# One of four sample tiles gets its first expert products from gathered rows and VectorE dots

## The chip, the cores and the metric

The kernel runs on one core of a Trainium2 chip. The metric is the device time of one launch in microseconds. Times are the median of several executions; the profile is one further execution. The engines are TensorE (PE; its weight loads are PEld), VectorE (DVE), ScalarE (ACT), GpSimd (POOL) and SyncE (SP), which issues most transfers.

## The reference

One layer runs for a prompt of 128 tokens and a sample of 512 tokens: adaLN modulation, a long-convolution half and a gated-linear-attention half, an output projection, then the PEER expert mixer. The change is in the mixer:

```python
def peer_ffn(h, wq, sub_keys, u_tab, v_tab):          # h2 of 128 + 512 tokens, D = 1024
    q = (x @ wq).reshape(T, 8, 2, 128)
    s = einsum('thpd,hpkd->thpk', q, sub_keys)         # 128 sub-keys per half
    s_top, i_top = top_k(s, 16)
    cand_s = s_top[:, :, 0, :, None] + s_top[:, :, 1, None, :]
    best, pos = top_k(cand_s.reshape(T, 8, -1), 16)    # 16 experts of 16384 for each of 8 heads
    gate = softmax(best)
    ...
    a = gelu(einsum('td,tkd->tk', xt, u_tab[it]))      # 128 experts per token
    return einsum('tk,tkd->td', gt * a, v_tab[it])
```

All data is float32. Each token uses 8 x 16 = 128 of the 16384 experts; a row of `u_tab` or `v_tab` is 1024 numbers.

## The kernel before

There are five tiles of 128 tokens: tile 0 is the prompt, tiles 1 to 4 the sample. After the mixing half come, in order:

- **The query product** (L878, L879): the moving operand is 320 tokens wide, in a three-part split of each float32 (high by high, high by low, low by high). While it runs, DVE takes the top keys.
- **Stage A**, `BLK_A` = 40 blocks. A block is 128 experts. All 16384 experts, 128 blocks, are multiplied with the 512 sample tokens: `first_products` (L898 and on) makes 24 matmuls 128x512 a block (L906), after ACT has rounded the expert rows to `uhi` (L1672) and POOL has made the rest `ulo` (L1815). ACT takes the gelu of the block (L1682) to `aout`, which SP stores to `gelu_scratch` and then loads the rows of four blocks on. Meanwhile DVE finishes the top-k (`best_keys`, `best_experts`), first of the prompt, whose expert numbers `idx0` POOL waits for ahead of its ninth split; it issues four row gathers there.
- **Stage B**, 4 x 16 blocks. Besides the same products, PE makes one 128x128 product per sample token (L946) that scatters the token's 128 gates over its 16384 experts. DVE builds one operand `eA` of these (L1442, 8 a block) and ACT the other, `eB` (L1708, L1710); ACT copies the result to `gst`, which SP stores to `gate_scratch`. DVE now makes `ulo` too (L1417). For the prompt nothing is dense: POOL gathers the rows `u[idx]` of the 128 prompt tokens, one expert a token at a time (L1827, 128x1024), and DVE takes the dot with `h2row` (L1427), `DOTS_B` = 2 a block, 128 in all.
- **Stage C**, the remaining 24 blocks: only the first products.
- **Stage 2**, 128 blocks, 24 matmuls 128x512 a block (L965): gelu value times gate for 512 tokens (DVE L1459), its high and low parts, the high and low parts of the `v` rows, and the product. For the prompt POOL gathers a row of `v_tab` a token and DVE adds it (L1475), one a block.

Each engine works through its list in the order written; semaphores join them. Buffers that matter here: `ugat` and `vgat` have `GSLOT` = 4 slots (the gather of dot g+4 is issued once dot g is done), `uraw`, `vraw` and `ain` have four, `gin` holds four blocks' gates and there are two of it, `uhi` and `ulo` have two.

## Time and profile before

| | us |
|---|---|
| median of 3 executions | 2248.36 (2241.95 to 2249.47) |
| profiled execution, its own time | 2244.61 |
| its span | 2242.8 |
| mean granted clock of TensorE, share of full | 0.979 |

| engine | busy us | share of the span |
|---|---|---|
| PE | 2154.6 | 96% |
| DVE | 1388.6 | 62% |
| ACT | 834.1 | 37% |
| POOL | 508.7 | 23% |

The 16 transfer engines moved 475.50 MB. In the chain that ended last PE has 90% of the span: L965 (stage 2) 30%, L906 (first products) 29%, L946 (gate scatter) 5%. A share over the whole span says little here, because the stages have different limits; the rows below take one stage at a time. Times in them count from the start of the span.

### The profile page before, as it was taken

The numbers are of one execution on the slowest core, as the hardware profiler recorded it, in microseconds if no ns is written. First come the engines' busy times: TensorE is split into PE (matmuls) and PEld (weight loads), VectorE is DVE, ScalarE is ACT, GpSimd is POOL, SyncE is SP. The second block draws the span as 40 slices with busy tenths as digits, with TensorE's granted clock in tenths as the row PEclk, the third lists the DMA queues.
The fourth block names the chain that finished last, engine by engine and source line by source line (L and its number), as shares of the span: only waits on it lengthen the run. The fifth ranks groups of instructions, "written<-read, shape, count | busy, mean of one in ns | idle before, by whom it ended". The sixth has DMA issues, their size and how long they took to land.

```text
span 2242.8 us, 28983 instructions
## 1 busy us (share of the span) xinstructions
PE 2154.6 (96%) x9868; PEld 1664.0 (74%) x9868; DVE 1388.6 (62%) x2919; ACT 834.1 (37%) x1506; POOL 508.7 (23%) x329
## 2 busy tenths in 40 slices
PE   6999999698998999999999999999999999999998
PEld 2554455445997787788888888887888888888886
DVE  4221425423889999677777777226666666666665
ACT  2111003323212222677877877223222223223222
POOL 0000001002324555333333332003222222222120
PEclk8999999798999999999999999999999999999999
DMA  9121114305102444488888887747888888888883
GB/s 338 53 75 45 73 43 178 150 1 197 56 21 85 169 136 142 160 307 317 322 319 315 317 319 293 285 139 281 315 298 284 290 293 285 293 283 296 279 298 132
DMA packets 179297, 475.50 MB, mean 212 GB/s; under 512 B 16263, under 2 KB 50215, under 8 KB 176648
## 3 DMA queue, kind: packets, MB, share of 16 engines
q1 hardware_dynamic: 142344, 340.20, 42.7%
q0 software_dynamic: 36864, 134.23, 17.9%
q8 instruction: 42, 0.69, 0.1%
q14 instruction: 47, 0.39, 0.1%
HBM read 401.76 MB, written 72.61 MB: 212 GB/s over the span
## 4 chain that ended last, share of the span: by engine, by line
PE 90%; DVE 4%; DMA 2%; ACT 1%; issue 1%; POOL 1%; SPq 0%; POOLq 0%; DVEq 0%; ACTq 0%
PE ps L965 30%; PE ps L906 29%; PE ps L624 5%; PE ps L946 5%; PE ps L717 3%; PE ps L843 3%; PE ps L878 3%; PE ps L879 3%; PE ps L683 2%; DMA wring<-in_w_ada 1%; PE ps L623 1%; PE ps L636 1%; DMA ain<-gelu_scratch 1%; PE ps L742 1%; PE ps L743 1%
## 5 line engine op out<-in xcount | busy, mean ns | idle before, releaser
L906 PE MATMUL ps<-h2hi,uhi 128*128 128x512 f32 x1024 | 446.3, 436 | 18.5 <-DVE scores L1375 7.7
L965 PE MATMUL ps<-vhi,whi 128*128 128x512 f32 x1024 | 400.8, 391 | 8.1 <-DVE wlo L1465 8.1
L906 PE MATMUL ps<-h2hi,ulo 128*128 128x512 f32 x1024 | 402.8, 393 | 0.0
L906 PE MATMUL ps<-h2lo,uhi 128*128 128x512 f32 x1024 | 401.1, 392 | 0.0
L965 PE MATMUL ps<-vlo,whi 128*128 128x512 f32 x1024 | 400.2, 391 | 0.0
L965 PE MATMUL ps<-vhi,wlo 128*128 128x512 f32 x1024 | 399.9, 391 | 0.0
L1751 ACT ACTIVATE vhi<-vraw 128x1024 fp32r<-128x1024 f32 x128 | 135.5, 1061 | 471.4 <-PE ps L965 464.0
L1835 POOL DMA_INDIRECT vgat<-in_v_tab,idx x128 | 151.4, 1183 | 659.7 <-DVE y L1475 507.7
L1463 DVE TENSOR_TENSOR vlo<-vraw,vhi 128x1024 fp32r<-128x1024 f32 x128 | 156.9, 1226 | 215.8 <-ACT vhi L1751 215.8
L1827 POOL DMA_INDIRECT ugat<-in_u_rows,idx x128 | 176.9, 1382 | 287.4 <-DVE dots L1427 265.4
L1417 DVE TENSOR_TENSOR ulo<-uraw,uhi 128x1024 fp32r<-128x1024 f32 x87 | 106.7, 1226 | 200.8 <-ACT uhi L1672 200.8
L965 PEld LDWEIGHTS ps<-vhi,whi 128*128 128x128 f32 x1024 | 193.2, 189 | 49.5 <-issue 6.0
L906 PEld LDWEIGHTS ps<-h2hi,uhi 128*128 128x128 f32 x1024 | 195.2, 191 | 42.9 <-issue 16.5
L946 PEld LDWEIGHTS ps<-eA,eB 128*128 128x128 f32 x1024 | 192.8, 188 | 44.8
L906 PEld LDWEIGHTS ps<-h2hi,ulo 128*128 128x128 f32 x1024 | 193.1, 189 | 42.4
L965 PEld LDWEIGHTS ps<-vhi,wlo 128*128 128x128 f32 x1024 | 193.4, 189 | 40.4
L965 PEld LDWEIGHTS ps<-vlo,whi 128*128 128x128 f32 x1024 | 193.6, 189 | 40.1
L906 PEld LDWEIGHTS ps<-h2lo,uhi 128*128 128x128 f32 x1024 | 195.3, 191 | 19.5
L946 PE MATMUL ps<-eA,eB 128*128 128x128 f32 x1024 | 196.3, 273 | 0.0
L1682 ACT ACTIVATE aout<-ps 128x512 f32<-128x512 f32 x128 | 76.1, 595 | 256.2 <-PE ps L906 256.2
L1475 DVE SCALAR_TENSOR_TENSOR y<-vgat,w,y 128x1024 f32<-128x1024 f32 x127 | 162.5, 1279 | 0.8 <-DMA vgat<-in_v_tab,idx 0.8
L1427 DVE CUSTOM_DVE_ANT_0 junk<-ugat,h2row 128x1024 f32<-128x1024 f32 x128 | 156.6, 1224 | 2.2
(268 smaller groups left out, 2998.0 us busy)
## 6 DMA issues: line engine op xcount, KB each, us to landing
uraw<-in_u_t SPq DMA_DIRECT2D x128, 512.0 KB
vraw<-in_v_tab SPq DMA_DIRECT2D x128, 512.0 KB, 5.2
gelu_scratch<-aout SPq DMA_DIRECT2D x128, 256.0 KB
gate_scratch<-gst SPq DMA_DIRECT2D x16, 2048.0 KB
ain<-gelu_scratch SPq DMA_DIRECT2D x128, 256.0 KB, 4.2
gin<-gate_scratch SPq DMA_DIRECT2D x32, 1024.0 KB, 9.4
wring<-in_w_ada SPq DMA_DIRECT2D x12, 2048.0 KB, 9.3
wring<-in_w_in SPq DMA_DIRECT2D x6, 2048.0 KB, 8.3
```

The costliest lines, as they stand in the source:

```text
L624: s_ = pe.matmul(bank(us)[0:m], w, as_, start=(j == 0), stop=(j == n - 1))
L906: last = pe.matmul(ps[:, b % 4, :], w[:, b % 2, k, :], h[:, k, LP:T], start=(k == 0 and j == 0), stop=(k == KD - 1 and j == 2))
L946: pe.matmul(o_, eB[:, b % 2, k], eA[:, q % RING], start=True, stop=True).then_inc(onehot_used, 1)
L965: last = pe.matmul(ps[:, y_bank(t) + h, :], w[:, b, (t - 1) * P:t * P], v[:, b, h * 512:(h + 1) * 512], start=(start and j == 0), stop=(st ...
L1417: dve.tensor_tensor(ulo[:, b % 2], uraw[:, b % 4], uhi[:, b % 2].bitcast(F32), ALU.subtract).then_inc(ulo_ready, 1)
L1427: dve.tensor_tensor_reduce(junk[:], ugat[:, g % GSLOT], h2row[:], 1.0, 0.0, ALU.mult, ALU.add, dots[:, k:k + 1]).then_inc(dot_done, 1)
L1463: dve.tensor_tensor(vlo[:, s], vraw[:, s], vhi[:, s].bitcast(F32), ALU.subtract).then_inc(vlo_ready, 1)
L1475: dve.scalar_tensor_tensor(y0[:], vgat[:, s], w0[:, bass.ds(n, 1)], y0[:], ALU.mult, ALU.add).then_inc(v_added, 1)
L1682: act.activation(aout[:, b % 4], ps[:, b % 4, :], ACT.Gelu_apprx_tanh).then_inc(gelu_done, 1)
L1751: act.activation(vhi[:, s], vraw[:, s], ACT.Copy).then_inc(vhi_ready, 1)
L1827: pool.indirect_dma_start(out=ugat[:, k % GSLOT], out_offset=None, in_=u_rows, in_offset=bass.IndirectOffsetOnAxis(ap=idx0[:, k:k + 1], ax ...
L1835: pool.indirect_dma_start(out=vgat[:, k % GSLOT], out_offset=None, in_=v_tab, in_offset=bass.IndirectOffsetOnAxis(ap=idx0[:, k:k + 1], axis=0)
```

## The change

The first product is no longer dense for tile 4, the last sample tile (`TU`): the dense part covers 384 tokens (`TA`), so the matmuls of L906 become 128x384 and `aout` and `gelu_scratch` 384 wide. For tile 4 POOL gathers 128 expert rows and DVE takes 128 dots, as for the prompt. ACT takes their gelu, DVE multiplies it with the tile's gates, PE turns the result, and these weights take the place of the gates in tile 4's scatter, which is the last 16 blocks of stage B; in stage 2 this tile needs no product with a gelu value. So tile 4's dots must end ahead of block 47 of stage B. They take the first 45 blocks of stage B, 38 with three dots and 7 with two. The prompt's dots move behind them: two a block in the last 19 blocks of stage B, three a block in stage C, and the other 54 in stage 2, one or two a block. The prompt's value rows are then added in 89 blocks of stage 2, one or two a block. Stage 2's products keep their shapes. Stage A has 52 blocks, stage B 64 and stage C 12. The four early gathers stand ahead of POOL's 25th split and use tile 4's expert numbers, so all tiles' `best_keys` come ahead of them on DVE. Two more groups of four transposes, with their copies on ACT, make the prompt's `h2` in rows beside tile 4's. `ain` is loaded for four blocks at once from a scratch that is stored by partition, after each fourth `vraw`.

```diff
+TU = NT - 1
+TA = TD - P
-BLK_A = 40
+BLK_A = 52
-POOL_FROM = 8
+POOL_FROM = 24
+NDOT = 2 * HK
+U_LAST = 44
 DOTS_B = 2
-DOTS_IT = DOTS_B * NB_B
+DOTS_C = 3
+def dots_before(n):
+    m = n - BLK_A
+    if m <= U_LAST:
+        return -(-HK * m // (U_LAST + 1))
+    if n <= BLK_C:
+        return HK + DOTS_B * (m - U_LAST - 1)
+    d = dots_before(BLK_C)
+    if n <= NBLK:
+        return d + DOTS_C * (n - BLK_C)
+    return min(NDOT, d + DOTS_C * (NBLK - BLK_C) + 3 * (n - NBLK) // 2)
...
-    a_dram = nc.dram_tensor("gelu_scratch", [NBLK, P, TD], F32, kind="Internal").ap()
+    a_dram = nc.dram_tensor("gelu_scratch", [P, NBLK, TA], F32, kind="Internal").ap()
...
-                        last = pe.matmul(ps[:, b % 4, :], w[:, b % 2, k, :], h[:, k, LP:T],
+                        last = pe.matmul(ps[:, b % 4, 0:TA], w[:, b % 2, k, :], h[:, k, LP:LP + TA],
...
+                    if b == turn_after:
+                        pe.wait_ge(w0_ready, 1)
+                        pe.wait_ge(gelu_done, BLK_A + TURN_U - 1)
+                        pe.transpose(ps[:, TURN_BANK, 0:P], dots[:, 0, :], ident[:]).then_inc(w_turned, 1)
...
             for n in range(BLK_A, BLK_C):
                 m = n - BLK_A
+                if m == TURN_U + 1:
+                    dve.wait_ge(w_turned, 1)
+                    dve.tensor_copy(cols_hk[:, 2, TA:TD], ps[:, TURN_BANK, 0:P]).then_inc(w_taken, 1)
+                    dve.wait_ge(w_taken, 1)
...
-                for e in range(DOTS_B):
-                    dot(DOTS_B * m + e)
-            for n in range(BLK_C + 1, NBLK):
-                split_u(n, n)
+                if m == TURN_U:
+                    slot_weights(0)
+                for g in dots_at(n):
+                    dot(g)
+            for n in range(BLK_C, NBLK):
+                if n + 1 < NBLK:
+                    split_u(n + 1, n + 1)
+                for g in dots_at(n):
+                    dot(g)
...
+            for n in range(NBLK):
+                if n + 1 < NBLK:
+                    weight(n + 1)
+                low_parts(n)
+                for g in dots_at(NBLK + n):
+                    dot(g)
+                if n == GELU_P + 1:
+                    slot_weights(1)
+                for g in values_at(n):
+                    add_value(g)
```

How the instructions stand now. First DVE in stage B, one block; `ISA junk` is a dot, the row behind it takes out its sum, and the names in brackets are the semaphores waited for. Before:

```order
L1442 TENSOR_SCALAR eA<-iota,cols_hk 128x128 [waits onehot_used] x5
L1417 TENSOR_TENSOR ulo<-uraw,uhi 128x1024 [waits h_full,uhi_ready]
L1442 TENSOR_SCALAR eA<-iota,cols_hk 128x128 [waits onehot_used] x3
L1427 ISA junk,dots<-ugat,h2row 128x1024 [waits u_gathered2,dot_done]
L1427 ISA dots 128x1
L1427 ISA junk,dots<-ugat,h2row 128x1024 [waits u_gathered3,dot_done]
```

The same place now:

```order
L1495 TENSOR_SCALAR eA<-iota,cols_hk 128x128 [waits onehot_used] x5
L1469 TENSOR_TENSOR ulo<-uraw,uhi 128x1024 [waits h_full,uhi_ready]
L1495 TENSOR_SCALAR eA<-iota,cols_hk 128x128 [waits onehot_used] x3
L1477 ISA junk,dots<-ugat,h2row_u 128x1024 [waits u_gathered3,dot_done]
L1477 ISA dots 128x1
L1477 ISA junk,dots<-ugat,h2row_u 128x1024 [waits u_gathered0,dot_done]
L1477 ISA dots 128x1
L1477 ISA junk,dots<-ugat,h2row_u 128x1024 [waits u_gathered1,dot_done]
```

A third dot stands between a block's `eA` and the next block's.

Then DVE at the end of stage B, in stage C and at the start of stage 2. Before:

```order
L1427 ISA junk,dots<-ugat,h2row 128x1024 [waits u_gathered3,dot_done]
L1427 ISA dots 128x1
L1417 TENSOR_TENSOR ulo<-uraw,uhi 128x1024 [waits h_full,uhi_ready] x23
L1434 TENSOR_TENSOR w_113<-acur,gate_114 128x32 [waits dots_gelu]
L1459 TENSOR_TENSOR ain<-ain,gin_117 128x512 [waits g_landed0,a_landed0]
```

One block of stage C now:

```order
L1469 TENSOR_TENSOR ulo<-uraw,uhi 128x1024 [waits h_full,uhi_ready]
L1477 ISA junk,dots<-ugat,h2row_p 128x1024 [waits u_gathered2,dot_done]
L1477 ISA dots 128x1
L1477 ISA junk,dots<-ugat,h2row_p 128x1024 [waits u_gathered3,dot_done]
L1477 ISA dots 128x1
L1477 ISA junk,dots<-ugat,h2row_p 128x1024 [waits u_gathered0,dot_done]
```

Stage C had only splits on DVE; now three dots stand behind each.

Last POOL, from the end of its splits on. Before:

```order
L1846 COMPARE_AND_BRANCH
L1815 TENSOR_TENSOR ulo<-uraw,uhi 128x1024 [waits h_full,uhi_ready]
L1827 DMA ugat<-in_u_rows,idx_110 128x1024 [waits dot_done] x124
L1835 DMA vgat<-in_v_tab,idx_110 128x1024 [waits h_full]
L1835 DMA vgat<-in_v_tab,idx_110 128x1024 x3
L1835 DMA vgat<-in_v_tab,idx_110 128x1024 [waits v_added] x124
```

Now:

```order
L1874 TENSOR_TENSOR ulo<-uraw,uhi 128x1024 [waits h_full,uhi_ready]
L1884 DMA ugat<-in_u_rows,idxs 128x1024 [waits dot_done,idx_ready]
L1884 DMA ugat<-in_u_rows,idxs 128x1024 [waits dot_done] x251
L1892 DMA vgat<-in_v_tab,idxs 128x1024 [waits h_full]
L1892 DMA vgat<-in_v_tab,idxs 128x1024 x3
L1892 DMA vgat<-in_v_tab,idxs 128x1024 [waits v_added] x124
```

256 gathers of first rows where there were 128, through the same four slots; the value gathers follow all of them.

## Rows read from the trace of the kernel before

**Rows 1.** Timeline of PE: first matmul of stages A, B and 2.

```profile
687.88 0.76 PE L906 MATMUL ps<-h2hi,uhi 128*128 128x512 f32 x1 [7.74 <-DVE scores L1375]
...
923.66 0.47 PE L906 MATMUL ps<-h2hi,uhi 128*128 128x512 f32 x1 [2.61 <-issue]
...
1527.55 0.47 PE L965 MATMUL ps<-vhi,whi 128*128 128x512 f32 x1 [2.13 <-DVE wlo L1465]
```

**Rows 2.** Chain that ended last: start us, us, what; stages A, C and 2.

```profile
738.41 0.23 issue
...
1394.83 130.61 PE ps L906 x576
...
1548.68 660.10 PE ps L965 x2904
```

**Rows 3.** Stretches: busy us by engine, PE clock, transfer engines' share, GB/s.

```profile
core 0: us, PE busy (x) PEld busy (x) DVE busy (x) ACT busy (x) POOL busy (x), PEclk, DMA share, GB/s
...
716.00:720.00 4.00, 3.14 (x15) 2.26 (x14) 3.99 (x1) 1.55 (x2) 2.97 (x2) 1.00 0.23 88
...
1100.00:1200.00 100.00, 100.00 (x547) 85.88 (x546) 76.70 (x178) 80.24 (x179) 38.72 (x28) 1.00 0.90 332
...
1700.00:1900.00 200.00, 200.00 (x884) 165.68 (x883) 132.89 (x148) 58.19 (x74) 42.42 (x37) 1.00 0.88 289
```

**Rows 4.** Timeline of PE in the query product: 320 columns.

```profile
674.23 0.31 PE L878 MATMUL ps<-h2hi,qwhi 128*128 128x320 f32 x1
...
675.11 0.31 PE L878 MATMUL ps<-h2hi,qwhi 128*128 128x320 f32 x1
```

**Rows 5.** Timeline of ACT and POOL in stage A: one block's split.

```profile
701.31 0.60 ACT L1682 ACTIVATE aout<-ps 128x512 f32<-128x512 f32 x1 [3.89 <-PE ps L906]
...
702.93 2.40 POOL L1815 TENSOR_TENSOR ulo<-uraw,uhi 128x1024 fp32r<-128x1024 f32 x1 [3.05 <-ACT uhi L1672]
```

**Rows 6.** Groups by shape: POOL's splits, all 41.

```profile
L1815 POOL TENSOR_TENSOR ulo<-uraw,uhi 128x1024 fp32r<-128x1024 f32 x41 | 116.6, 2846 | 134.8 <-ACT uhi L1672 134.7
```

**Rows 7.** Timeline of POOL, DVE and PE near the early gathers.

```profile
713.81 4.41 POOL L1815 TENSOR_TENSOR ulo<-uraw,uhi 128x1024 fp32r<-128x1024 f32 x1 [3.04 <-ACT uhi L1672]
...
716.01 4.36 DVE L1367 TENSOR_TENSOR oneh<-oneh,itopf 128x2048 f32<-128x2048 f32 x1
...
738.64 0.49 PE L906 MATMUL ps<-h2hi,uhi 128*128 128x512 f32 x1 [3.22 <-POOL ulo L1815]
```

**Rows 8.** Timeline of DVE in stage B: one block.

```profile
1100.59 1.37 DVE L1442 TENSOR_SCALAR eA<-iota,cols_hk 128x128 f32<-128x128 f32 x5
...
1103.60 1.23 DVE L1417 TENSOR_TENSOR ulo<-uraw,uhi 128x1024 fp32r<-128x1024 f32 x1 [1.64 <-ACT uhi L1672]
...
1105.50 1.23 DVE L1427 CUSTOM_DVE_ANT_0 junk<-ugat,h2row 128x1024 f32<-128x1024 f32 x1
...
1107.92 1.37 DVE L1442 TENSOR_SCALAR eA<-iota,cols_hk 128x128 f32<-128x128 f32 x5
```

**Rows 9.** Timeline of POOL in the same block: gathers issued.

```profile
1107.01 1.80 POOL L1827 DMA_INDIRECT ugat<-in_u_rows,idx  x1 [4.24 <-DVE dots L1427]
...
1109.12 0.98 POOL L1827 DMA_INDIRECT ugat<-in_u_rows,idx  x1 [0.30 <-issue]
```

**Rows 10.** Stretches in stage B while gates are stored: columns as rows 3.

```profile
1107.30:1114.60 7.30, 7.30 (x41) 6.29 (x40) 5.63 (x14) 5.88 (x14) 2.76 (x3) 1.00 1.00 409
1114.60:1122.00 7.40, 7.40 (x42) 6.33 (x41) 5.73 (x14) 5.98 (x14) 2.86 (x3) 1.00 1.03 424
```

**Rows 11.** Issue of transfers, 1700 to 1800 us: count, KB, us to landing.

```profile
vgat<-in_v_tab,idx POOLq DMA_INDIRECT x19, 5.0
```

**Rows 12.** Timeline at the start of stage 2: third value gather and its addition.

```profile
1528.42 0.94 POOL L1835 DMA_INDIRECT vgat<-in_v_tab,idx  x1 [0.31 <-issue]
...
1538.20 1.28 DVE L1475 SCALAR_TENSOR_TENSOR y<-vgat,w,y 128x1024 f32<-128x1024 f32 x1 [0.20 <-DMA vgat<-in_v_tab,idx]
```

**Rows 13.** Timeline of ACT ahead of the query product.

```profile
538.81 0.60 ACT L1518 ACTIVATE h2row<-ps 128x512 f32<-128x512 f32 x1 [0.26 <-PE ps L614]
```

More of the change, by code:

```diff
@@ L854, in _ @@
                 ada_cols(i)
-            for h in range(2):
-                transposes(f"hr{h}", [h2T[:, 4 * h + j, 0:P] for j in range(4)])
+            for x, t in (("u", TU), ("p", 0)):
+                for h in range(2):
+                    transposes(f"h{x}{h}", [h2T[:, 4 * h + j, rows(t)] for j in range(4)])
             pe.wait_ge(ld_keys, 16)
@@ L1382, in _ @@
             wait_gate_rows(1)
-            best_experts(0)
-            seq(dve.scalar_tensor_tensor(work[:, 9], selw[:, 0, 0], float(NKEYS), selw[:, 0, 1], ALU.mult, ALU.add))
-            dve.tensor_copy(idx0[:], work[:, 9]).then_inc(idx_ready, 1)
             for t in range(T_EARLY, NT):
@@ L1389, in _ @@
                     best_keys(t, h)
-            for t in range(1, NT):
+            dve.wait_ge(h2row_ready, 1)
+            for x, t in enumerate((TU, 0)):
+                best_experts(t)
+                seq(dve.scalar_tensor_tensor(work[:, 9], selw[:, t, 0], float(NKEYS), selw[:, t, 1], ALU.mult, ALU.add))
+                dve.tensor_copy(idxs[:, x], work[:, 9]).then_inc(idx_ready, 1)
+            for t in range(1, TU):
                 best_experts(t)
@@ L1476, in add_value @@
+            def add_value(g):
+                s = g % GSLOT
+                dve.wait_ge(v_gathered[s], 16 * (g // GSLOT + 1))
+                if g == 0:
+                    dve.wait_ge(w0_ready, 2)
+                    dve.tensor_scalar(y0[:], vgat[:, s], dots[:, 1, 0:1], None, ALU.mult).then_inc(v_added, 1)
+                else:
+                    dve.wait_ge(v_added, g)
+                    dve.scalar_tensor_tensor(y0[:], vgat[:, s], dots[:, 1, g:g + 1], y0[:], ALU.mult, ALU.add
                                              ).then_inc(v_added, 1)
-            def step_2(it, first, last):
-                for b in range(TOPK):
-                    n = it * TOPK + b
-                    if not (last and b == TOPK - 1):
-                        weight(it, b + 1)
-                    low_parts(n, b % R2)
-                    add_value(it, b, first)
@@ L1640, in _ @@
             for h in range(2):
-                move(f"hr{h}", h2row[:, h * 512:(h + 1) * 512])
+                move(f"hu{h}", h2row[0][:, h * 512:(h + 1) * 512])
+            act.wait_ge(h2lo_ready, NT)
+            wait_unit(act, "hp1")
+            for h in range(2):
+                move(f"hp{h}", h2turn[:, h * 512:(h + 1) * 512])
             def split_q(h):
@@ L1663, in _ @@
                     gate_rows(1)
+            wait_drained(act, "hp1")
+            act.wait_ge(x1_stored, 16)
+            act.activation(h2row[1][:], h2turn[:], ACT.Copy).then_inc(h2row_ready, 1)
             def split_u(n, b, first):
@@ L1710, in slot_keys, with slot_gelu @@
                 act.activation(eB[:, m % 2], eB[:, m % 2], ACT.Relu, bias=1.0, scale=-1.0).then_inc(onehot_j_ready, 1)
-            def slot_gelu(r, first):
-                act.wait_ge(dot_done, DOTS_IT * (r + 1))
-                if not first:
-                    act.wait_ge(w0_ready, r)
-                act.activation(acur[:], dots[:], ACT.Gelu_apprx_tanh).then_inc(dots_gelu, 1)
+            def slot_gelu(x):
+                act.wait_ge(dot_done, HK * (x + 1))
+                act.activation(dots[:, x], dots[:, x], ACT.Gelu_apprx_tanh).then_inc(dots_gelu, 1)
             for b in range(4):
@@ L1735, in step_b @@
                     split_u(n + 1, b + 1, False)
-                    if b == 0 and not first:
-                        slot_gelu(it - 1, second)
+                    if n == BLK_A + GELU_U:
+                        slot_gelu(0)
                     if n + 1 < BLK_C:
@@ L1759, in _ @@
                     split_u(n + 1, (n + 1) % 4, False)
-                if n == BLK_C + 1:
-                    slot_gelu(NTD - 1, False)
                 if n == NBLK - 1:
                     for b in range(R2):
-                        high_v(b, b, 16, True)
+                        high_v(b)
                 gelu(n, n % 4, False)
-            def step_2(it, first):
-                for b in range(TOPK):
-                    n = it * TOPK + b
-                    if not (first and b < R2):
-                        high_v(n, b % R2, it * 64 + 16 * (b // R2 + 1), False)
-                    high_w(n, b % R2)
-            loop(act, IT_2, step_2)
+            for n in range(NBLK):
+                if n >= R2:
+                    high_v(n)
+                high_w(n)
+                if n == GELU_P:
+                    slot_gelu(1)
             for t in range(NT):
```

165 lines of the change are left out of this document (84 added, 81 removed).

## The prediction, made before the changed kernel was run

> **What bounds the kernel now.** I read the stages one by one. First the first matmuls of the stages [rows 1] and the chain of waits [rows 2]: stage A runs from 687.88 to 923.66 (235.8 us), stage B from there to 1394.8 (471.2 us, 7.36 a block), stage C 130.6 us (576 matmuls, 24 blocks, 5.44 a block, 0.2268 a matmul), stage 2 from 1527.55 on. The stretches [rows 3] show PE busy throughout in stages B and 2, with DVE at 77% and 66%, ACT at 80% and 29%. So PE sets the pace of all three, and a shorter first product helps as far as DVE, which gets all the new work, and the transfers let it. In stage B the transfer engines have a share of 0.90 at 332 GB/s already.
>
> **A matmul of 384 columns.** No row has one. 320 columns in the same split: six matmuls from 674.23 to 675.11, 0.147 each [rows 4]; 512 columns 0.2268. The straight line between is 0.417 ns a column and gives 0.173, so 1.28 us less for a block's 24: 4.16 in stages A and C, and in stage B, where a block repeats every 7.33 (eA to eA, [rows 8]), 6.05.
>
> **Ahead of stage A.** Four more transposes a half and two more copies on ACT precede the query product; a copy there takes 0.60 and waited 0.26 for its transposes [rows 13]: two are +1.7, on the path. The copy of the prompt's rows to their place falls in the 7.74 us for which PE waits for DVE [rows 1]: nothing.
>
> **Stage A.** 52 blocks of 4.16 are 216 us, 40 of 5.44 were 218. But another loop is as long: from the gelu's start at 701.31 through ACT's split to the end of POOL's at 705.33 is 4.02 us [rows 5], and with a matmul's start 0.23 behind its split [rows 2] it allows a block every 4.25. That is +3 over 52 blocks, and the slack of 1.2 us that this loop had a block is gone. In it lay POOL's long splits: mean 2846 ns against 2400 undisturbed, 18.3 us over 41 [rows 5, 6]. They come from pairs like the one at 713.81, where POOL needs 4.41 and DVE's multiplication right behind 4.36 [rows 7]; both have neighbours of 2.4 and 2.3. What was hidden is now on the path: between nothing and all 18.3, times 5.44/4.25 for denser splits, so 0 to 23; two in a row overlap, I take 14. The four early gathers held PE up by 3.22 less the slack [rows 7]; without the slack +2. DVE's top-k ends close to PE's stage A as before. Sum +19 (5 to 31).
>
> **Stage B, first 45 blocks (331 us before).** Three limits lie together.
> DVE: a block has 5.69 us of work (7.33 less the 1.64 waited); a dot is 1.21 (1105.50 to 1107.92 are two) [rows 8]. With three dots 6.90. 38 such blocks and 7 of two dots at PE's 6.05 are 305 us, 6.8 a block. The work on ACT, 5.9 us a block, stays below.
> Transfers: an expert block in (0.524 MB), gelu out (0.197), gates out (0.524) and 2.84 gathers of 0.524 are 2.74 MB. While gates are stored the engines move 409 and 424 GB/s at shares of 1.00 and 1.03 [rows 10]: at 415 a block needs 6.6.
> The ring of four gather slots: dot g, the issue of gather g+4 that waits for the next dot to leave (1.80 against 0.98, [rows 9]), the landing, dot g+4. That is the landing plus 2.4 us for four dots. A landing takes 5.0 in the middle of stage 2 [rows 11] and 9.8 when much is under way (issued 1528.42, used 1538.20, DVE having waited 0.20) [rows 12]. So one dot each 1.85 to 3.05 us, a block 5.3 to 8.7.
> Three of eight blocks have a gate store beside them, where the ring sets some 7.8 (landing about 8.6); the others 6.8. Mean 7.2: 324 us, -7 (305 to 390).
> Here stands one rule of the Trainium skill against this trace: DMA: Bandwidth & Descriptors, the section on the anatomy of one DMA, puts a transfer issued by GpSimd at about 2.0 us plus its bytes over 436 GB/s, an estimate of 3.2 for a gather. By it the ring would give a dot each 1.4 us and never bind; rows 11 and 12 say 5.0 and more.
>
> **Stage B, last 19 blocks (140 us).** Two dots: DVE 5.69, transfers 2.29 MB or 5.5, PE 6.05. With an occasional wait 6.2: 118 us, -22. The turned weights add a wait of PE ahead of block 47 for a small product on DVE, done a block before; if late, the block's matmuls stand behind it, a microsecond in all.
>
> **Stage C (130.6 us).** 12 blocks. PE 4.16, DVE 1.2 + 3 x 1.21 = 4.8, POOL three issues of 1.0 to 1.8. Transfers: 36 gathers, 8 expert blocks, 12 gelu stores, the last gates (4.2 MB) and stage 2's first loads (3.9 MB), 33.6 MB in all or 81 us at 415. Not all must land before stage 2; between 58 us (DVE) and 82. I take 6.0 a block, 72 us: -59.
>
> **Stage 2.** PE keeps its 24 matmuls. DVE has 132.89 us of work in 200, 3.6 a block [rows 3]; less one addition (1.2 beside its neighbours, [rows 12]), plus 1.5 dots: 4.2, later 4.1 with 1.44 additions. Below 5.45 (24 of 660.10 / 2904, [rows 2]). Transfers: 289 GB/s is 1.57 MB a block; half a gather more and a quarter less of `ain` is 1.77 MB, 324 GB/s. The row's own share says 289/0.88 = 328 at full share, so the cover is thin: 0, with up to +25 if loads come late, and -6 if the first loads, now made in stage C, save the wait at its start.
>
> **Sum.** 1.7 + 19 - 7 - 22 - 59 + 0 = -67. The profiled execution's own time is 2244.6, so 2177; the median shown stands 3.8 higher, so the prediction is 2181.
>
> **Rivals.**
> 1. Gathers land in time. The gate stores of before cost DVE nothing, and its only wait in the block shown is for ACT [rows 8]. Then B's first part is 306 (-25), C 60 (-71), and POOL's collisions mostly overlap (+8): 1.7 + 8 - 25 - 22 - 71 = -108, 2140. Against it: before, a gather had two blocks' time.
> 2. The transfer engines are full. Over 100 us of stage B they moved 332 GB/s at a share of 0.90, 369 at a full one [rows 3]. Then 7.41 in the first part (+3), C 91 us (-40): 1.7 + 19 + 3 - 22 - 40 = -38, 2210. Against it, 409 and 424 over seven microseconds each [rows 10].
> The Trainium skill, SBUF — State Buffer, the section on its two separate sides, gives about 358 GB/s between HBM and a core. By it the parts would be 344, 122 and 94 us, and the time 2227. Rows 10 stand above that figure, so it gets no chance beyond rival 2's.
> 3. Slower: the ring of four slots sets the pace at the longest landing, 9.8 us, because the 45 blocks keep the engines near full and each gather queues behind loads and stores. One dot each 3.05 us: first part 390 (+59), last part unchanged (-22), C 36 x 3.05 = 110 (-21), with +19 and +1.7: +37, 2285. It decides from a mean landing of 8.9 us (164 dots at 2.82 us fill what they replace). For it: the one gather seen in traffic. Against: 5.0 at a share of 0.88.
> 4. The matmul does not get shorter with its columns. Then stages A and B would be slower by over 60 us. The 320-column row excludes it.
>
> **How the numbers follow.** The forecast 0.48, rival 1 0.24, rival 2 0.14, rival 3 0.14. The terms' own ends (A 5 to 31, B 305 to 390, C 58 to 82, stage 2 -6 to +25) reach further than any one case; 8 in 10 lie from rival 1's side, 2135, to beyond rival 2, 2240; what is left out is mostly rival 3. This kernel's measurement tells 0.3%, 6.7 us, from no change. Faster by more 0.84, within it 0.04 (rival 3 near its point of decision), slower 0.12.
>
> **What would show it.** L906's matmuls 0.173 apart in stage C and PE's block in the last 19 of stage B near 6.1. In stage A, PE waits for POOL's `ulo` of 10 to 20 us in sum, where one of 3.22 stood out. In stage B's first part PE waits for `eA` of about a microsecond a block, and DVE idles for gathered rows beside gate stores only; if in nearly every block, rival 3. A granted clock that falls in those waits would be against me: a stretch with PE busy 3.14 of 4 us kept 1.00 [rows 3]. Stage C near 72 us with DVE waiting for rows, not for `uhi`. In stage 2 no waits past the first blocks. A stage A that ends more than 35 us later, or a first part over 8 us a block, makes the prediction wrong.

## The result, and the profile after

The changed kernel takes 2261.78 us (median of 9, 2251.13 to 2263.11), the kernel before 2245.63 (median of 9, 2241.95 to 2249.63): ratio 1.0059 (the median over all pairs of executions), 95% interval 1.0043 to 1.0075. It is slower by 0.6%. The forecast was 2181 us with a range from 2135 to 2240: it said 67 us less, there are 16 more, and the time lies outside the range. The profiled execution took 2262.82 us, its span is 2261.0 (before 2242.8), the mean granted clock 0.955 (before 0.979).

By the start of each block's gelu on the timeline of ACT the span divides so (before and after in us; a stage is counted from the gelu of the last block ahead of it to that of its own last block, stage A from its first gelu):

| stretch | before | after | difference | forecast |
|---|---|---|---|---|
| to the first gelu | 695.9 | 699.5 | +3.6 | +1.7 |
| stage A | 225.2 | 240.2 | +15.0 | +19 |
| stage B, first 45 blocks | 334.9 | 388.6 | +53.7 | -7 |
| stage B, last 19 blocks | 139.3 | 127.8 | -11.6 | -22 |
| stage C | 130.1 | 84.2 | -45.9 | -59 |
| from the last gelu on | 717.3 | 720.8 | +3.5 | 0 |

Of the 86 us by which the rows miss in all, 61 are in one. The next fence has the stretches of the changed kernel, with the columns of [rows 3]: stage B, stage C, the start of stage 2, the middle of stage 2.

```profile
core 0: us, PE busy (x) PEld busy (x) DVE busy (x) ACT busy (x) POOL busy (x), PEclk, DMA share, GB/s
943.00:1300.00 357.00, 283.64 (x1674) 275.63 (x1673) 278.18 (x614) 241.31 (x537) 160.66 (x119) 0.89 0.86 313
1456.00:1540.00 84.00, 59.02 (x286) 56.79 (x284) 51.87 (x76) 20.34 (x28) 41.01 (x33) 0.84 0.99 380
1545.00:1600.00 55.00, 49.45 (x211) 40.83 (x212) 49.25 (x75) 15.18 (x20) 22.31 (x19) 0.92 1.02 399
1700.00:1900.00 200.00, 200.00 (x884) 165.59 (x883) 145.01 (x173) 58.07 (x75) 69.13 (x50) 1.00 0.88 311
```

Where PE was busy throughout in stage B before [rows 3], it is busy 283.64 of 357 us now, and DVE, which has the added work, only 278.18. Neither is the bound, and the transfer engines move 313 GB/s at a share of 0.86, less than the 332 at 0.90 before the change. All of them wait. In the middle of stage 2 PE is busy all the time, as forecast.

The waits from 943 to 1330 us (us in total, times, longest). "issue" means that the profile names nothing that PE waited for:

```profile
PE ps L985 <- issue: 78.1, 30, 8.2
DVE junk L1477 <- DMA ugat<-in_u_rows,idxs: 59.2, 26, 7.5
DVE ulo L1469 <- ACT uhi L1736: 25.4, 14, 3.9
```

What begins the circle is DVE's wait for gathered rows: 59.2 us in 26 waits. Before, no gather held DVE in the block shown [rows 8], nor anywhere from 943 to 1250 us, where this is DVE's only wait:

```profile
DVE ulo L1417 <- ACT uhi L1672: 68.7, 42, 1.6
```

The dots of two such blocks of the changed kernel on DVE, the counterpart of [rows 8]:

```profile
977.86 1.22 DVE L1477 CUSTOM_DVE_ANT_0 junk<-ugat,h2row_u 128x1024 f32<-128x1024 f32 x1
...
979.13 1.22 DVE L1477 CUSTOM_DVE_ANT_0 junk<-ugat,h2row_u 128x1024 f32<-128x1024 f32 x1
...
980.39 1.22 DVE L1477 CUSTOM_DVE_ANT_0 junk<-ugat,h2row_u 128x1024 f32<-128x1024 f32 x1
...
984.74 1.22 DVE L1477 CUSTOM_DVE_ANT_0 junk<-ugat,h2row_u 128x1024 f32<-128x1024 f32 x1
...
985.99 1.22 DVE L1477 CUSTOM_DVE_ANT_0 junk<-ugat,h2row_u 128x1024 f32<-128x1024 f32 x1
...
989.10 1.23 DVE L1477 CUSTOM_DVE_ANT_0 junk<-ugat,h2row_u 128x1024 f32<-128x1024 f32 x1 [1.88 <-DMA ugat<-in_u_rows,idxs]
990.25 0.08 DVE L1477 DVE_READ_ACCUMULATOR2_ANT dots<- 128x1 f32 x1
990.25 1.40 DVE L1495 TENSOR_SCALAR eA<-iota,cols_hk 128x128 f32<-128x128 f32 x5
```

And POOL at the same time, the counterpart of [rows 9]:

```profile
979.36 1.80 POOL L1884 DMA_INDIRECT ugat<-in_u_rows,idxs  x1 [4.03 <-DVE dots L1477]
981.47 0.97 POOL L1884 DMA_INDIRECT ugat<-in_u_rows,idxs  x1 [0.30 <-issue]
982.74 2.12 POOL L1884 DMA_INDIRECT ugat<-in_u_rows,idxs  x1 [0.30 <-issue]
```

With four slots, the dot of 989.10 uses the slot that the dot of 979.13 freed at 980.28, four dots before. POOL is still issuing the gather before it and issues this one at 981.47; it is there at 989.10, 7.6 us on. The three dots of a block stand in a row, so from the end of the second of one block to the third of the next is one block and one dot, not the four thirds of a block that four dots are on the mean. And `eA` of the next block stands behind the late dot (990.25). The same place in short stretches, columns as above, the first two around that wait and the last three beside gate stores:

```profile
987.00:990.00 3.00, 1.20 (x8) 0.88 (x6) 1.12 (x3) 2.29 (x5) 1.97 (x2) 1.00 0.85 270
990.00:993.00 3.00, 2.30 (x9) 2.33 (x10) 3.00 (x10) 2.97 (x8) 0.94 (x1) 0.64 1.01 355
1012.00:1016.00 4.00, 0.21 (x2) 0.00 (x0) 0.00 (x0) 3.97 (x11) 0.98 (x2) 0.84 1.03 434
1016.00:1020.00 4.00, 0.00 (x0) 0.00 (x0) 1.22 (x3) 1.06 (x1) 0.00 (x0) 0.50 0.98 398
1020.00:1024.00 4.00, 3.62 (x13) 3.65 (x14) 4.00 (x12) 0.00 (x0) 0.94 (x1) 0.50 1.06 445
```

PE is out of work at 988, and its granted clock, 1.00 from 987 to 990, is 0.64 from 990 to 993: partly at the lower of its levels, 1.2 GHz. Beside the gate stores PE stands still for eight microseconds and then works at 0.50, wholly at the lower level. The transfer engines move 434, 398 and 445 GB/s there, and DVE waits 7.5 us, up to its dot of 1018.78. That dot uses the slot of the dot of 1003.13. The rows, from several views: the issue of its gather on POOL, the two gate stores on SP, who waited for this gather (us, times), and its time from issue to landing:

```profile
1005.48 0.96 POOL L1884 DMA_INDIRECT ugat<-in_u_rows,idxs  x1 [0.30 <-issue]
1005.85 0.45 SPq L573 DMA_DIRECT2D gate_scratch<-gst  x1
1014.10 0.51 SPq L573 DMA_DIRECT2D gate_scratch<-gst  x1
  DVE junk L1477: 7.5, 1
DMA to landing us min/median/max: 13.2/13.2/13.2
```

It was issued 0.4 us ahead of the first gate store and 8.6 ahead of the second, and still took 13.2 us: large stores hold back a gather that is already under way, too. How long transfers took from issue to landing, 1000 to 1300 us (count, KB, median us):

```profile
gate_scratch<-gst SPq DMA_DIRECT2D x10, 2048.0 KB, 14.2
uraw<-in_u_t SPq DMA_DIRECT2D x34, 512.0 KB, 6.9
ugat<-in_u_rows,idxs POOLq DMA_INDIRECT x99, 6.6
```

A gather takes 6.6 us at the median, not the 5.0 of [rows 11]. Counted one by one in the trace, of the 128 gathers issued during the first 45 blocks 44 were under way together with a gate store and took 10.3 us on the mean; the other 84 took 6.2, the longest 8.6. Over all the mean is 7.6. The blocks of the first 45 are 10.2, 6.0 and 7.7 us long, over and over, with one of 12 to 16.5 about every eighth; 8.6 on the mean.

### The profile page after: what moved, and what is told of

Same layout as the page of the kernel before. It is cut to its first block, busy times and chain, and to the rows that moved or that the text cites. A ratio compares the mean times of both kernels' runs of the same rounds, so it can differ in the third digit from the quotient of the medians.

```text
span 2261.0 us, 28461 instructions
## 1 busy us (share of the span) xinstructions
PE 2044.0 (90%) x9877; PEld 1659.8 (73%) x9877; DVE 1527.1 (68%) x3164; ACT 823.9 (36%) x1507; POOL 734.7 (32%) x469
## 4 chain that ended last, share of the span: by engine, by line
PE 82%; issue 6%; DMA 4%; ACT 3%; DVE 3%; POOL 1%; SPq 0%; ACTq 0%; POOLq 0%; DVEq 0%
PE ps L1012 31%; PE ps L945 20%; PE ps L985 5%; PE ps L662 5%; PE ps L755 3%; PE ps L881 3%; PE ps L917 3%; PE ps L918 3%; PE ps L721 2%; DMA uraw<-in_u_t 2%; DMA wring<-in_w_ada 1%; PE ps L661 1%; ACT gst L1762 1%; POOL ulo L1874 1%; PE ps L780 1%
## 5 line engine op out<-in xcount | busy, mean ns | idle before, releaser
L1884 POOL DMA_INDIRECT ugat<-in_u_rows,idxs x256 | 338.8, 1323 | 448.9 <-DVE dots L1477 416.0
L945 PE MATMUL ps<-h2hi,uhi 128*128 128x384 f32 x1024 | 409.5, 400 | 49.8 <-issue 28.9
L945 PE MATMUL ps<-h2lo,uhi 128*128 128x384 f32 x1024 | 358.3, 350 | 0.0
L945 PE MATMUL ps<-h2hi,ulo 128*128 128x384 f32 x1024 | 355.3, 347 | 0.0
L985 PE MATMUL ps<-eA,eB 128*128 128x128 f32 x1024 | 211.3, 290 | 89.5 <-issue 84.2
L1892 POOL DMA_INDIRECT vgat<-in_v_tab,idxs x128 | 192.4, 1503 | 301.9 <-DVE y L1534 263.7
L1477 DVE CUSTOM_DVE_ANT_0 junk<-ugat,h2row_u 128x1024 f32<-128x1024 f32 x128 | 156.4, 1222 | 61.2 <-DMA ugat<-in_u_rows,idxs 59.2
L1477 DVE CUSTOM_DVE_ANT_0 junk<-ugat,h2row_p 128x1024 f32<-128x1024 f32 x128 | 156.4, 1222 | 43.0 <-DMA ugat<-in_u_rows,idxs 41.7
L1874 POOL TENSOR_TENSOR ulo<-uraw,uhi 128x1024 fp32r<-128x1024 f32 x53 | 139.7, 2639 | 123.7 <-ACT uhi L1736 123.7
L1534 DVE SCALAR_TENSOR_TENSOR y<-vgat,dots,y 128x1024 f32<-128x1024 f32 x127 | 162.5, 1280 | 5.5 <-DMA vgat<-in_v_tab,idxs 1.7
## 6 DMA issues: line engine op xcount, KB each, us to landing
gin<-gate_scratch SPq DMA_DIRECT2D x32, 1024.0 KB, 12.2
```

The costliest lines, as they stand in the source:

```text
L945: last = pe.matmul(ps[:, b % 4, 0:TA], w[:, b % 2, k, :], h[:, k, LP:LP + TA], start=(k == 0 and j == 0), stop=(k == KD - 1 and j == 2))
L985: pe.matmul(o_, eB[:, b % 2, k], eA[:, q % RING], start=True, stop=True).then_inc(onehot_used, 1)
L1477: dve.tensor_tensor_reduce(junk[:], ugat[:, g % GSLOT], h2row[x][:], 1.0, 0.0, ALU.mult, ALU.add, dots[:, x, k:k + 1]).then_inc(dot_done, 1)
L1534: dve.scalar_tensor_tensor(y0[:], vgat[:, s], dots[:, 1, g:g + 1], y0[:], ALU.mult, ALU.add).then_inc(v_added, 1)
L1874: pool.tensor_tensor(ulo[:, b % 2], uraw[:, b % 4], uhi[:, b % 2].bitcast(F32), ALU.subtract).then_inc(ulo_ready, 1)
L1884: pool.indirect_dma_start(out=ugat[:, g % GSLOT], out_offset=None, in_=u_rows, in_offset=bass.IndirectOffsetOnAxis(ap=idxs[:, g // HK, g % ...
```

## The experiments

Theories. **T1**: a ring of four slots, with dots in a clump of three on DVE, does not cover a landing of 6.6 us. **T2**: the transfer engines are full, whatever the ring. **T3**: DVE's own work, or TensorE's fallen clock, holds the blocks. Each kernel below is the changed kernel (2261.78) with the edit named. The stretches are counted as in the table above, from one profiled execution each; that of e3 was 8 us below its kernel's median, that of e10 11 us above. The kernel before, run again beside each group, stayed between 2243.9 and 2246.6 us. e1 and e5 leave out data and compute other results, as said there:

| kernel | time | A | B first 45 | B last 19 | C |
|---|---|---|---|---|---|
| changed | 2261.8 | 240.2 | 388.6 | 127.8 | 84.2 |
| e1 no gathers (1 run) | 2150.9 | 242.9 | 313.0 | 118.7 | 60.7 |
| e2 spread | 2221.4 | 240.9 | 351.4 | 128.5 | 88.1 |
| e3 smooth | 2244.8 | 240.9 | 373.6 | 119.0 | 87.9 |
| e4 six slots | 2218.6 | 240.9 | 346.7 | 128.5 | 86.5 |
| e5 half rows (1 run) | 2195.0 | 240.9 | 339.7 | 120.5 | 74.6 |
| e6 wide (1 run) | 2313.4 | 289.5 | 379.2 | 139.8 | 86.5 |
| e8 spread, six | 2193.3 | 240.8 | 324.6 | 130.1 | 84.1 |
| e9 e8, 1 dot in C | 2174.8 | 240.8 | 324.7 | 132.3 | 70.3 |
| e10 e9, spread in first 45 only | 2173.8 | 242.9 | 325.6 | 131.5 | 74.9 |
| e11 e10, smooth | 2144.7 | 241.0 | 306.4 | 118.8 | 68.0 |
| e12 e10, no dot in C | 2169.5 | 240.9 | 323.6 | 133.1 | 66.9 |
| e13 e11 with four slots | 2159.6 | 243.0 | 317.4 | 118.8 | 68.4 |

### e1: the gathers taken out

```diff
-                dve.wait_ge(u_gathered[g % GSLOT], 16 * (g // GSLOT + 1))
+                dve.wait_ge(u_gathered[g % GSLOT], 16)
...
-            for g in range(GSLOT, NDOT):
-                gather_u(g)
```

> Only the first four gathers of rows of u are issued; the 256 dots stay, all on these four slots, and none waits for a gather. It leaves out the other 252 gathers, so the weights of the last tile are not computed. Theories: T1, the ring of four slots (landing 5 to 8 us and longer beside gate stores) holds the clump of three dots at the end of each block; T2, the transfer engines are full in stage B; T3, what holds stage B is VectorE's own work (three dots and nine other operations a block, 6.8 us) or TensorE's fallen clock, whoever makes it wait. T1 and T2: the first 45 blocks of stage B go from 388.6 us to about 305 (6.8 us a block), stage C from 84 to about 58, the whole from 2262 to about 2150. T3 with VectorE as the limit: the first 45 blocks stay within 15 us of 388.

2150.85 us. The first 45 blocks take 313.0 us, stage C 60.7; 76 and 24 us of the changed kernel are its gathers. The stretch as before:

```profile
943.00:1300.00 357.00, 325.47 (x2103) 313.66 (x2104) 340.67 (x761) 301.91 (x679) 0.00 (x0) 1.00 0.51 177
```

DVE is now busy 340.67 of 357 us and the blocks are 6.9 us, as its work says. So DVE's own time, sized right in the prediction, is not what holds the changed kernel. T3's first half is out. TensorE's granted clock stays at 1.00 here, though PE is without work for 31.5 of the 357 us; its fall in the changed kernel goes with the longer waits.

### e2: the dots spread among the eA

```diff
...
-                for g in dots_at(n):
-                    dot(g)
...
+                    if k in (1, 4, 7)[3 - len(dots_at(n)):]:
+                        dot(dots_at(n)[(1, 4, 7)[3 - len(dots_at(n)):].index(k)])
```

> The dots of a block stand among its eight squaring operations (behind the second, fifth and eighth) instead of in a row at the block's end; nothing else changes. If the clump is the trouble (T1: three dots in a row free three slots within 4 us and then nothing for 4 us, and the next block's splits stand behind the last dot), even spacing gives each gather some 7 us from request to use: the first 45 blocks of stage B fall from 388.6 us to 310 to 350 and the time to 2190 to 2225. If the transfer engines are full (T2) the bytes are the same and the blocks stay at 8 to 8.6 us: 2255 to 2265. If the number of slots alone counts (four slots over a landing of 6.6 us plus 2.4), the mean block does not change either, since four slots pass at the same rate however the dots are placed.

2221.35 us; against the kernel before 0.9886 (0.9853 to 0.9918). The first 45 blocks go from 388.6 to 351.4. Slots, bytes and number of gathers are the same, so neither the mean pace of the ring nor full engines alone were the limit: the place of the dots was worth 37 us. The waits for rows, same stretch as before:

```profile
DVE junk L1477 <- DMA ugat<-in_u_rows,idxs: 40.8, 23, 6.0
```

The time is at the less good end of what T1 gave, and the first 45 blocks are just past its 350; what is left are mainly blocks of 8 to 14 us beside gate stores, most others are 6.7.

### e3: gate stores in eight pieces

```diff
-                ii = slice(64 * part_, 64 * part_ + 64)
+                ii = slice(16 * part_, 16 * part_ + 16)
...
-                    elif b == HALF:
-                        store_g(it * 2, 0, 1)
+                    elif HALF <= b < NB_B - 1:
+                        store_g(it * 2, 0, b - HALF + 1)
```

> Each half of the gate buffer goes to DRAM in eight pieces of 16 columns of the loop instead of two of 64, one piece a block; bytes are the same. If the bursts of the gate stores make the long blocks (13.8 to 16.5 us every eighth block, against 8.0 for the others), these vanish: 5 or 6 blocks of 45 lose some 6 us each, 25 to 35 us, and the time falls to 2230 to 2240. If bytes alone count (T2), the long blocks go but the others get longer: within 8 us of 2262. If the smaller pieces (short rows in DRAM) cost the transfer engines more, slower than 2262.

2244.80 us, 0.9992 (0.9974 to 1.0010): 17 us below the changed kernel where 22 to 32 were expected, and 373.6 in the first 45 blocks. The blocks of 13.8 to 16.5 us are gone, but nine take 11.3 to 13.1 now, where the changed kernel has two of 12.2. That a burst spread out touches more blocks, where clump and four slots leave each at the edge, is my reading; no run takes it apart.

### e4: six slots

```diff
-        ugat = at("ugat", 0, [P, GSLOT, D])
+        ugat = [at(f"ugat{b}", k, [P, D]) for b, k in enumerate((0, 4, 8, 12, 20, 24))]
...
+            sp_.dma_start(g2_dram, g2row[:].rearrange("p s d -> p (s d)")).then_inc(g2_saved, 16)
...
-                if g >= GSLOT:
-                    pool.wait_ge(dot_done, g - GSLOT + 1)
+                if g >= GU:
+                    pool.wait_ge(dot_done, g - GU + 1)
```

> Six slots for the gathered rows of u instead of four; the room for two more comes from sending the second norm's scale rows (1 MB) to DRAM ahead of stage A and reading them back behind the last dot, of no weight for the time. If the ring is the limit (T1), a gather may take 1.5 times as long before it holds a dot: the first 45 blocks of stage B fall from 388.6 us to about 315 (7 us a block, VectorE's own work), stage C from 84 to 62 to 75, the time to 2165 to 2190. If the transfer engines are full (T2), six in flight land later in the same proportion and the blocks stay at 8.6: 2255 to 2265.

2218.60 us, 0.9886 (0.9850 to 0.9921): as much as the spread, by the other factor of T1. It fell short of T1's 2165 to 2190, and T2's "no change" is wrong too. The waits for rows fall to less than half:

```profile
DVE junk L1488 <- DMA ugat<-in_u_rows,idxs: 26.7, 18, 3.4
```

### e5: half the bytes a gather

```diff
-                pool.indirect_dma_start(out=ugat[:, g % GSLOT], out_offset=None, in_=u_rows,
+                half = g >= GSLOT
+                pool.indirect_dma_start(out=ugat[:, g % GSLOT, 0:512] if half else ugat[:, g % GSLOT], out_offset=None,
+                                        in_=u_rows.rearrange("r (a c) -> (r a) c", a=2) if half else u_rows,
```

> The gathers behind the first four bring 512 columns of a row (2 KB a partition, 0.26 MB) instead of 1024; their number, issue, slots and order stay, and the dots read all 1024 columns, the second half being that of the slot's first gather. The weights of the last sample tile and the prompt's first products are therefore others. Two causes are to be told apart that the spread dots and the six slots both relieved: how long a gather takes because of its bytes on shared transfer engines (B), or because of a fixed time from issue to landing with four in flight (F). B: landing falls well below 6.6 us, the first 45 blocks of stage B go from 388.6 to 305 to 320 us, the whole to 2150 to 2175. F: landing stays above 5.5 us and the first 45 blocks above 350, the whole above 2215.

2194.96 us, the first 45 blocks 339.7: between the two. Landing:

```profile
ugat<-in_u_rows,idxs POOLq DMA_INDIRECT x95, 5.3
```

Half the bytes shorten a landing only from 6.6 to 5.3 us, with the engines at a share of 0.74 in place of 0.86 (943 to 1300 us). A line through both gives 4.0 us for no bytes; it is drawn through two loads of the engines, so it is an estimate and says only that most of a landing is not the gather's own bytes. The bytes are worth 49 of the 76 us; blocks of 10 to 14 us beside gate stores remain.

### e6: the first products 512 wide again

```diff
-                        last = pe.matmul(ps[:, b % 4, 0:TA], w[:, b % 2, k, :], h[:, k, LP:LP + TA],
+                        last = pe.matmul(ps[:, b % 4, :], w[:, b % 2, k, :], h[:, k, LP:T],
```

> The first products are 512 columns wide again, as before the change, for all 128 blocks (tile 4's results of them go unused); all else is as in the changed kernel, the gathers, dots and their order too. What the narrower product is worth where it stands: if the gathers alone set stage B (a block's length does not depend on TensorE), its first 45 blocks stay at 380 to 395 us, stage C at 80 to 90, and only stage A (52 blocks, +1.05 to 1.2 each) gets longer, by 55 to 62 us, the last 19 blocks by 10 to 20: 2325 to 2345. If TensorE's waits with its clock at half are themselves a cause (the clock's fall makes blocks longer, which delays the splits), a busier TensorE keeps its clock and the first 45 blocks get shorter, 340 to 370: 2290 to 2320.

2313.36 us. That lies in the second range, but not for its reason; the pieces tell them apart. Against the changed kernel stage A is 49 us longer where 55 to 62 were expected, the last 19 blocks 12, stage C 2, and the first 45 blocks are 9 us shorter, 379.2: a microsecond below the first range and 9 above the second. So in those 45 blocks 128 fewer columns in 24 matmuls a block gain nothing: their length is set by the gathers.

```profile
943.00:1300.00 357.00, 331.03 (x1685) 274.78 (x1684) 257.68 (x569) 232.79 (x510) 146.86 (x113) 0.97 0.81 290
```

The clock is granted at 0.97 here and at 0.89 in the changed kernel, and the first 45 blocks are 9 us shorter, net of the wider products and in one execution. The waits of DVE give a second view. A slow PE can hold DVE only where DVE waits, and from 943 to 1300 us the changed kernel has two kinds of wait, for rows and for ACT's `uhi`; ACT works in order and waits for PE in between. In e1, with its clock at 1.00, the second kind is 13.1 us over the same stretch. In the changed kernel:

```profile
DVE junk L1477 <- DMA ugat<-in_u_rows,idxs: 53.2, 24, 7.5
DVE ulo L1469 <- ACT uhi L1736: 21.5, 13, 2.7
```

The difference of the second kind is 8.4 us. So the fallen clock (T3) can be some 10 us of the 54, an estimate from e6 and these waits; a kernel that changes the clock alone was not run.

### e8: spread and six slots

Edits of e2 and e4 together.

> Both remedies together: dots among the squaring operations of the block, and six slots. Each alone took 40 us off the changed kernel. With six slots alone the transfer engines have a share of 0.94 at 349 GB/s from 943 to 1330 us, with the spread alone 0.93 at 343. If the engines are now the limit, the two do not add: the first 45 blocks of stage B, 345 us with the one and 340 with the other, stay at 325 to 340, and the time is 2205 to 2220. If waits for rows remain the limit, they add: first 45 blocks at 305 to 315 us, 2180 to 2195.

2193.32 us, 0.9778 (0.9761 to 0.9796). The first 45 blocks are 324.6: e2 took 37 off and e4 42, both 64. They add in large part. (The expectation has 340 for e2's first 45 blocks; by the table it is 351.4.) The landing with six in flight:

```profile
ugat<-in_u_rows,idxs POOLq DMA_INDIRECT x99, 10.0
```

It is longer than the 6.6 of the changed kernel, with six in flight where there were four and the engines at a share of 0.98; a longer landing beside fewer waits. A landing is not a constant to compare slots with.

### e9: one dot a block in stage C

```diff
-DOTS_C = 3
+DOTS_C = 1
```

> As the one before with one dot a block in stage C instead of three; the 24 others go into stage 2, which has 78 of them in 52 blocks. Stage C's 12 blocks take 84 to 88 us in the changed kernel and the two remedies, TensorE's own work there is 50 us, and the transfers have a share of 0.99. If the gathers in C crowd out the expert blocks (uraw) and the first loads of stage 2, C falls to 60 to 70 us, and stage 2, with a share of 0.88 to 0.93, takes the 24 gathers at no cost or up to 5 us: 15 to 25 us below the kernel with three. If it is stage 2's loads that fill the transfers there, no gain: within 5 us of it.

2174.75 us, 0.9687 (0.9671 to 0.9704), 19 us below e8. Stage C takes 70.3 us instead of 84.1, and stage 2 has 24 dots more at no cost. The prediction's three dots a block in C took transfers from what C waits for.

### e10, e11, e12: three variants of e9

e10 spreads the dots in the first 45 blocks only; e11 adds the pieces of e3; e12 is e10 with `DOTS_C = 0`.

```diff
+                    if m <= U_LAST and k in (1, 4):
+                        g = dots_before(n + 1) - (3 if k == 1 else 2)
+                        if g >= dots_before(n):
+                            dot(g)
...
-                for g in dots_at(n):
+                for g in range(dots_before(n + 1) - 1 if m <= U_LAST else dots_before(n), dots_before(n + 1)):
                     dot(g)
```

> The fastest kernel so far (six slots, one dot a block in stage C), with the dots among the squaring operations only in the 45 blocks that have three; the last 19, with two a block, have them in a row at the end again, since spread blocks there took 6.7 us and blocks with the dots at the end 6.0 and 6.5 in turn. If those 6.7 come from a dot that stands ahead of the sixth to eighth eA, the last 19 blocks fall from 133 us by 6 to 9, and the time to 2164 to 2171. If it is a wait that the transfers set, the same 2175 within 3.

2173.83 us, 0.9674 (0.9650 to 0.9698): the same as e9. The blocks of 6.7 us did become 6.0 and 6.5 in turn, but three of the last 19 take 8.8, 10.3 and 11.6 us beside gate stores and the sum is 131.5.

> The same with each gate half stored in eight pieces. In the changed kernel the pieces took 17 us off, with four slots. Left in the first 45 blocks are some six long ones beside gate stores, 1 to 6 us over the others, 16 us in all. If pieces still help, 8 to 14 us less: 2155 to 2160. If, with the engines at a share of 0.97 and 366 GB/s, only bytes count now and smaller pieces cost more of them, no gain or up to 10 us slower than its neighbour without them.

2144.74 us, 0.9558 (0.9538 to 0.9579), 29 us below e10 and more than twice what was expected. It beats both kernels: 4.4% below the kernel before, 5.2% below the changed one. The first 45 blocks take 306.4 us, the last 19 118.8, all but a few 6.0 to 6.8. The pieces differ from e10's by more than the medians do, since its profiled execution took 11 us more than its median. Stage B, 943 to 1250 us, first of e10, then of e11:

```profile
943.00:1250.00 307.00, 275.31 (x1733) 259.54 (x1733) 282.03 (x635) 250.09 (x561) 120.69 (x125) 0.99 0.98 372
```

```profile
943.00:1250.00 307.00, 285.57 (x1834) 271.41 (x1834) 295.65 (x668) 266.43 (x598) 121.75 (x129) 1.00 1.01 393
```

At 372 GB/s the share was 0.98 already, and yet 393 were to be had; smaller pieces cost nothing that these two runs show. One block on DVE's timeline in e11, with the three dots (`junk`) apart; `ulo` and `eA` stand between them:

```profile
1009.83 1.21 DVE L1490 CUSTOM_DVE_ANT_0 junk<-ugat,h2row_u 128x1024 f32<-128x1024 f32 x1
1010.97 0.08 DVE L1490 DVE_READ_ACCUMULATOR2_ANT dots<- 128x1 f32 x1
1010.97 0.86 DVE L1508 TENSOR_SCALAR eA<-iota,cols_hk 128x128 f32<-128x128 f32 x3
1011.75 1.22 DVE L1482 TENSOR_TENSOR ulo<-uraw,uhi 128x1024 fp32r<-128x1024 f32 x1
1012.89 1.21 DVE L1490 CUSTOM_DVE_ANT_0 junk<-ugat,h2row_u 128x1024 f32<-128x1024 f32 x1
1014.03 0.08 DVE L1490 DVE_READ_ACCUMULATOR2_ANT dots<- 128x1 f32 x1
1014.03 0.87 DVE L1508 TENSOR_SCALAR eA<-iota,cols_hk 128x128 f32<-128x128 f32 x3
1014.82 1.21 DVE L1490 CUSTOM_DVE_ANT_0 junk<-ugat,h2row_u 128x1024 f32<-128x1024 f32 x1
```

No wait for rows is left between 943 and 1250 us. This is DVE's bound, which the prediction put at 305 us.

> As the first of these three, with no dot in stage C and 90 in the first 60 blocks of stage 2. One dot a block instead of three took 16 us off stage C and cost stage 2 nothing. Stage C takes 70 us against TensorE's 50; if the 12 gathers left are part of the 20, it falls to 60 to 65 and the time by 5 to 10 us. If the last gate store and stage 2's first loads (8 MB in 70 us) hold it, no change within 3 us.

2169.52 us, 0.9654 (0.9633 to 0.9675): 4 us below e10, with intervals that overlap; stage C 66.9 against 74.9, the last 19 blocks and stage 2 3.7 longer together. Not told apart.

### e13: four slots in the fastest kernel

> The fastest kernel (2145 us) with four slots for the gathered rows again instead of six; dots among the squaring operations, gate stores in eight pieces and one dot a block in stage C stay. It tells what the slots are worth once the clump and the bursts are gone. Four slots pass three dots each 6.7 us as long as a gather lands within 8.9 us less the 2.4 for dot and issue, 6.5 us, and the mean landing in the changed kernel was 6.6 to 7.1. If that holds: the first 45 blocks at 310 to 325 us against 307, the time 2148 to 2165. If the engines at full share let gathers land in 8 us and more whatever the slots (10 us was seen with six slots), four slots set 3 x (8 + 2.4) / 4 = 7.8 a block: 350 us, and 2185 to 2195.

2159.58 us, 0.9620 (0.9591 to 0.9649). The first 45 blocks are 317.4 us: with dots apart and stores in pieces four slots hold 6.7 us in half of the blocks and up to 7.6 in nearly all others, and six are worth 15 us more. The waits for rows are down from 59.2:

```profile
DVE junk L1479 <- DMA ugat<-in_u_rows,idxs: 10.2, 19, 2.7
```

T2's form of it (four slots at full engines give 7.8 a block) is wrong: the share is 0.98 at 373 GB/s from 943 to 1250 us, and the blocks are 7.1 on the mean, the first one of 10.9 among them. The expectation put the mean landing in the changed kernel at 6.6 to 7.1; counted in the trace it is 7.6.

## Why the prediction was wrong

**The failed step** is the stage B term for the first 45 blocks, -7 forecast and +54 measured, and in it the sentence "that is the landing plus 2.4 us for four dots". It spaces the dots evenly. By it a block of 6.9 us allows a landing of 4/3 x 6.9 - 2.4 = 6.8 us. But the order printed ahead of the prediction showed the three dots in a row. Then the second and third dot wait for gathers whose slots came free one block and one dot earlier. From the rows above: the dot before (1.2), the time to the issue behind POOL's other gather (1.2), the landing, less the one dot (1.2): a block is the landing plus 1.2, and 6.9 us allow 5.7. The 84 gathers without a gate store beside them took 6.2 on the mean: on the mean, evenly spaced dots would have let them pass, and the clump doesn't. Spreading the dots (e2) took 37 us off with nothing else changed, and brought most blocks away from gate stores to 6.7 us, which shows the place of the dots; slots (e4, 42), bytes (e5, 49) and bursts (e3, 15; 19 between e10 and e11) are the other factors of the same wait, and they overlap: alone they sum to more than the 76 that all gathers cost (e1).

**The landing** was the second size that was off. I took about 8.6 beside gate stores; the 44 gathers there took 10.3 on the mean and up to 16.6. After e2 the blocks beside gate stores still kept the first 45 at 351 us where 324 was forecast. Blocks without a gate store failed too, which the forecast had at no wait: DVE waited for rows 26 times in the 387 us shown, some 45 blocks, which is between the forecast's two signs ("beside gate stores only" and "in nearly every block, rival 3"). The 5.0 came from stage 2 at a share of 0.88, with one gather a block; here three stand behind one another.

**Rival 3** named the ring, though not the clump, with a price of +59 for the first 45 blocks; +53.7 was measured. It had a chance of 0.14. That its price came so near is luck: it was worked out from a landing of 9.8 us at even spacing. There 8.6 us a block want a landing of 9.1, the clump wants 7.4, and the mean of all 128 gathers was 7.6. It forecast 110 us for stage C and 84 was measured, so its total, 2285, is too high.

**Rival 2** (full engines at 369 GB/s) is out: 372 and 393 GB/s ran through whole stretches in e10 and e11. A rate divided by its share is no ceiling. The 358 GB/s that the Trainium skill, SBUF — State Buffer, in its section on the two separate sides, gives for this path is below both. By the Trainium skill, DMA: Bandwidth & Descriptors, the section on the anatomy of one DMA, a gather would take an estimated 3.2 us; among the other transfers of stage B the median measured is 6.6.

**Rival 1** (gathers in time, 2140) is what e11 reached, 2144.7, only after the order of the dots, the slots, the pieces and stage C's dots were changed.

**The other terms.** Stage A: +15 for +19 (its range should have ended at 28 and not 31, by its own terms), and POOL's splits there are 2656 ns on the mean against 2400 undisturbed, 13 us over 50, where 14 were taken. Ahead of A +3.6 for +1.7; the first gelu varied between 691.5 and 699.5 us in the kernels of this study, so a difference of 2 tells nothing. Last 19 blocks: -11.6 for -22; in e3, e11 and e13, with small pieces, they take 119, for the 118 forecast, and without gathers (e1) 118.7, so the missing 9 us are gate stores beside gathers, a cover that the sum had at "an occasional wait". Stage C: -46 for -59. With a share of 0.99 at 380 GB/s the 84 us are what the forecast's upper end of 82 said; I took 72. A matmul of 384 columns is 0.173 apart, as worked out, here in stage C:

```profile
1456.91 0.33 PE L945 MATMUL ps<-h2hi,uhi 128*128 128x384 f32 x1
1457.09 0.33 PE L945 MATMUL ps<-h2lo,uhi 128*128 128x384 f32 x1
1457.26 0.33 PE L945 MATMUL ps<-h2hi,ulo 128*128 128x384 f32 x1
```

Stage 2: 0 forecast, +3.5 measured. The chain that ended last passes these pieces at the end of stage C and the start of stage 2 (start us, us, what):

```profile
1509.92 12.35 DMA uraw<-in_u_t
1530.25 6.02 DMA ugat<-in_u_rows,idxs
1540.13 6.11 DMA ugat<-in_u_rows,idxs
```

An expert block comes late in C, and then the prompt's gathers hold DVE, on which stage 2's first `wlo` waits. With fewer dots in C (e9) the part from the last gelu on is 710.8 us instead of 716.3 in e8, though it has 24 dots more.

**The clock** fell in the waits, which the prediction had named as against it; by e6 and DVE's waits this can be some 10 us of the 54.

**What stays open:** how much of those 10 us is the clock, why small pieces help less with four slots and a clump (e3), and what sets the 4 us of a landing that are not the gather's bytes.

## What to carry to other kernels

For a ring of buffers, find the tightest reuse in the order as written: from the use that frees a slot to the use that needs it, less the issue. The mean pace is no bound when the uses stand in a clump on an in-order engine; spreading them gave 37 us in the blocks with three dots. It was not free everywhere: in the blocks with two, spread dots made 6.7 us where a row made 6.0 and 6.5 (e2, e10). When a stage gains transfers, look at the size of single stores as well as at bytes: beside stores of 2 MB a gather took 10.3 us on the mean, 6.2 elsewhere, even one issued just ahead of the store. Work moved into a stage should go where transfers have room, not where an engine has (one dot a block in stage C beat three by 19 us).
